# RMS norms summed into full banks on every partition, with the opening's work and its weight panels in a new order

## The reference

```python
def _rmsnorm(x, w):
    xf = x.astype(jnp.float32)
    y = xf * lax.rsqrt(jnp.mean(xf * xf, axis=-1, keepdims=True) + EPS)
    return (y * w.astype(jnp.float32)).astype(x.dtype)

def prep(t, use_rope):        # the first mixer, for the tokens and for the context
    rq, rk, rv, rg, mq, mk, mv, mo, mg = jnp.split(t @ w_in, AB_SPLITS, axis=-1)
    ...                       # heads, rope on rq and rk, a short convolution on mq and mk, gates
```

## Time and profile before

| | us |
|---|---|
| median of 3 runs (2335.64 to 2337.13) | 2336.91 |
| the profiled execution | 2333.99 |
| its span | 2332.2 |
| PE busy | 2236.8 (96%) |
| DVE busy | 1052.4 (45%) |
| ACT busy | 449.4 (19%) |
| POOL busy | 110.2 (5%) |

### The profile page before, as it was taken

How to read it: one execution, slowest core, us unless ns; L and a number is a source line. 1 busy time by engine, 2 the same in 40 slices (tenths; PEclk the granted TensorE clock), 3 DMA queues, 4 the chain that set the end, 5 groups by cost and what they waited for, 6 DMA issues and landing times.

```text
span 2332.2 us, 39035 instructions
## 1 busy us (share of the span) xinstructions
PE 2236.8 (96%) x16791; PEld 1627.1 (70%) x16791; DVE 1052.4 (45%) x2007; ACT 449.4 (19%) x1063; POOL 110.2 (5%) x103
## 2 busy tenths in 40 slices
PE   6989999999999999999999989999999999999997
PEld 4434454478886786678888668888775877777775
DVE  5488465478888335854431454441334520000001
ACT  1310242200000003630000351000332321111101
POOL 0210120000000420000000000000003000000000
PEclk9999999999999999999999999999999899999999
DMA  8424632244554324037885416886534158899994
GB/s 286 161 97 144 214 112 73 72 145 145 174 188 116 97 95 154 1 109 252 293 266 154 150 61 216 288 277 175 189 109 146 46 194 323 301 331 330 331 345 181
DMA packets 306217, 428.13 MB, mean 184 GB/s; under 512 B 11604, under 2 KB 166867, under 8 KB 305803
## 3 DMA queue, kind: packets, MB, share of 16 engines
q1 hardware_dynamic: 303412, 422.55, 53.2%
q10 hardware_dynamic: 2646, 3.26, 0.4%
HBM read 424.55 MB, written 1.13 MB: 183 GB/s over the span
## 4 chain that ended last, share of the span: by engine, by line
PE 90%; DVE 6%; ACT 1%; issue 1%; DMA 1%; ACTq 0%; SPq 0%; DVEq 0%
PE banks L645 76%; PE banks L905 3%; DVE mem L1846 2%; PE banks L654 1%; ACT mem L2871 1%; DVE mem L1849 1%; PE banks L1635 1%; PE banks L1039 1%; PE banks L1459 1%; DVE mem L1842 1%; PE banks L1074 1%; DVE mem L2438 1%; PE banks L1699 1%; PE banks L869 1%; PE banks L1081 0%
## 5 line engine op out<-in xcount | busy, mean ns | idle before, releaser
L645 PE MATMUL banks<-mem 128*32 128x128 f32 (+5 forms) x12722 | 1817.1, 359 | 21.6 <-ACT mem L2871 10.9
L645 PEld LDWEIGHTS banks<-mem 128*128 128x128 f32 (+3 forms) x12722 | 1308.2, 148 | 502.8 <-issue 296.6
L1846 DVE SCALAR_TENSOR_TENSOR mem<-mem 128x512 f32<-128x512 f32 (+4 forms) x523 | 376.9, 746 | 22.1 <-DMA mem<-mem 7.8
L2871 ACT ACTIVATE mem<-banks 128x256 f32<-128x256 f32 (+8 forms) x383 | 152.1, 419 | 1103.1 <-PE banks L645 804.3
L2871 ACT ACTIVATE mem<-mem 128x256 f32<-128x256 f32 (+11 forms) x445 | 192.0, 482 | 662.0 <-DVE mem L1846 469.5
L1849 DVE TENSOR_TENSOR mem<-mem,banks 128x256 f32<-128x256 f32 (+3 forms) x88 | 43.3, 492 | 561.8 <-ACT mem L2871 536.6
L1846 DVE SCALAR_TENSOR_TENSOR mem<-banks,mem 128x256 f32<-128x256 f32 (+7 forms) x258 | 133.6, 543 | 344.8 <-PE banks L645 227.5
L1849 DVE TENSOR_TENSOR mem<-mem 128x256 f32<-128x256 f32 (+13 forms) x272 | 153.5, 576 | 35.2 <-ACT mem L2871 19.8
L1849 DVE TENSOR_TENSOR mem<-banks,mem 128x256 f32<-128x256 f32 (+3 forms) x224 | 90.9, 410 | 101.9 <-PE banks L645 43.9
L654 PE MATMUL banks<-mem 128*128 128x128 f32 (+2 forms) x391 | 61.1, 293 | 24.1 <-DMA mem<-in_ctx 11.3
L654 PEld LDWEIGHTS banks<-mem 128*128 128x128 f32 (+2 forms) x391 | 46.0, 150 | 51.0 <-issue 22.8
(11 more groups left out here) (180 smaller groups left out, 826.6 us busy)
## 6 DMA issues: line engine op xcount, KB each, us to landing
mem<-in_ada_w SPq DMA_DIRECT2D x96, 1024.0 KB, 9.9
mem<-in_moe_w_gate_up SPq DMA_DIRECT2D x64, 1024.0 KB, 10.7
mem<-in_ffn_w_in SPq DMA_DIRECT2D x44, 1024.0 KB, 6.9
mem<-in_moe_w_down SPq DMA_DIRECT2D x48, 768.0 KB, 7.4
mem<-in_moe_w_gate_up SPq DMA_DIRECT2D x32, 768.0 KB, 12.6
mem<-in_ffn_w_out SPq DMA_DIRECT2D x32, 704.0 KB, 6.8
mem<-in_ffn_w_gate_up SPq DMA_DIRECT2D x22, 1024.0 KB, 6.4
mem<-in_ab_w_in SPq DMA_DIRECT2D x16, 1024.0 KB, 9.5
```

The lines of the kernel that those rows point to most:

```text
L645: ins = nc.tensor.matmul(o, lhsT, rhs, start=start, stop=stop)
L1846: return V.scalar_tensor_tensor(out=o, in0=a, scalar=sc, in1=b, op0=op0, op1=op1)
L2871: ac = lambda o, i, f, **k: nc.scalar.activation(o, i, f, **k)
```

## The change

- **Norms.** `norm_sum` now has the ones (128x128) as the stationary operand and the squares as the moving one, so that every partition gets the sums of all tokens in a full bank. Root and inverse run over all tokens (512 or 256 columns) on 128 partitions. `norm_spread` and the small matmul that opened the bank are gone; the scaling reads the inverse from `rms` (the former `rstd`) in place of a bank. The gain is computed ahead of the inverse.
- **Opening.** ACT squares each block as soon as it is copied, ahead of the SiLU. PE sums each of the eight squares itself (`sum_squares`, into bank 7), four of them between the last transposes and four after the packs; DVE's additions are gone. Both ada panels run back to back after that, and their two transposes follow each other. ACT loads the table for the root ahead of time.
- **Panels.** No ada panel is loaded or accumulated in the third panel (n = 2). Each later one moves one place back, and the last panel (n = 7) has two: one is summed after its second tile, and the accumulation of the other runs on DVE after that.

Left out of the diff: names of semaphores and counters, the rename of `rstd`, the other calls of `norm_spread`, and a second bank cleared at the start.

```diff
...
@@ -536,9 +536,9 @@
                 some_adas(2)
                 plain(w_in, [(512, 512), (4096, 32)])
                 some_adas(1)
-                for cc in (1024, 2048, 2560, 1536, 3584, 3072):
+                for cc, n in ((1024, 0), (2048, 1), (2560, 1), (1536, 2), (3584, 1), (3072, 2)):
                     plain(w_in, [(cc, 512)])
-                    some_adas(2 if cc == 1536 else 1)
+                    some_adas(n)
                 plain(A["ab_w_out"][0], [(0, 512), (512, 512)])
                 def spread_ctx(h):
...
@@ -728,26 +728,16 @@
             def norm_sum(width, src=hT, added=True, ends=(0, 7)):
-                m, tiles = c["nsq"], width // P
+                m = c["nsq"]
                 if added:
                     await_("norm_added", "nadd")
-                nc.tensor.matmul(PS[3][:, 0:tiles], const("ones", (HD, P)), const("ident", (HD, P))[:, 0:tiles], start=True, stop=True)
                 for k in (0, 7) if added else range(KD):
                     if k or not added:
                         pe.wait_ge(s["norm_squared"], m.n + k + 1)
-                    for i in range(tiles):
-                        b = ends[k // 7] if added else k
-                        last = nc.tensor.matmul(PS[3][:, i:i + 1], src[:, b, i * P:(i + 1) * P], const("ones")[:, 0:1],
-                                                start=False, stop=k == KD - 1, skip_group_check=True)
+                    b = ends[k // 7] if added else k
+                    last = nc.tensor.matmul(PS[3][:, 0:width], const("ones"), src[:, b, 0:width], start=k == 0, stop=k == KD - 1)
                 last.then_inc(s["sum_ready"], 1)
                 m.n += KD
-
-            def norm_spread(width):
-
-                await_("norm_inverted", "rooted")
-                for i in range(width // P):
-                    nc.tensor.matmul(PS[6 + i // 2][:, i % 2 * P:i % 2 * P + P], rstd[:, i:i + 1].to_broadcast([P, P]), ident,
-                                     start=True, stop=True).then_inc(s["norm_spread"], 1)
             pending = []
@@ -943,7 +933,7 @@
                     pe.wait_ge(s["blk_taken"], done + 3)
                     product(e, weights_of(w, 1, 1, q), blk.t4, more=True).then_inc(s["blk_ready"], 1)
-            def turn_x():
+            def turn_x(after):
                 pe.wait_ge(s["x_loaded"], 32)
                 for k in range(8):
@@ -952,22 +942,31 @@
                     for t in range(4):
                         last = turn(PS[k % 4][:, t * P:(t + 1) * P], xin[:, t, k * P:(k + 1) * P])
                     last.then_inc(s["x_turned"], 1)
+                    after(k)
+
+            def sum_squares(k):
+
+                pe.wait_ge(s["norm_squared"], k + 1)
+                last = mm(PS[7][:, :], const("ones"), hT[:, k, :], k == 0, k == 7)
+                if k == 7:
+                    last.then_inc(s["sum_ready"], 1)
+                    c["nsq"].n += KD
             pe.wait_ge(s["const_loaded"], 16)
-            turn_x()
+            turn_x(lambda k: sum_squares(k - 4) if k >= 4 else None)
             pe.wait_ge(s["vectors_loaded"], NVEC * 16)
             for g, pack in enumerate(PACKS):
                 n = sum(x for _, x in pack)
                 last = turn(PS[6][:, g * P:g * P + n], pack_rows[0:n, g, :])
             last.then_inc(s["packs_turned"], 1)
+            for k in range(4, 8):
+                sum_squares(k)
             pe.wait_ge(s["cond_ready"], 4)
-            ada()
-            ada_turned(2, c["ada"].n)
-            norm_sum(T2)
-            ada()
-            ada_turned(3, c["ada"].n)
+            for _ in range(2):
+                ada()
+            for i in (2, 3):
+                ada_turned(i, c["ada"].n - 1)
             if stop >= 1:
-                norm_spread(T2)
                 w = panel(8, 512)
                 def unshifted(b, after=lambda k: None):
@@ -1001,7 +1000,7 @@
                             project(w, slice(b * P, (b + 1) * P), T2)
                         else:
                             project_tok(w, b, slice(0, 512), 512)
-                        if n == 5 and b == 1:
+                        if n in (5, 7) and b == 1:
                             ada_sum(2, beside=True)
                         if n == 2:
@@ -1020,7 +1019,8 @@
                     if n == 1:
                         w = panel(8, 32)
                         project(w, slice(0, 32), T2, rows=(0, 32))
-                    ada_sum(2)
+                    if n != 2:
+                        ada_sum(2)
                 def spread_from(col):
...
@@ -1919,13 +1912,12 @@
             def last_adas():
-                ada_copied(3)
-                ada_biased(3)
+                for i in (2, 3):
+                    ada_copied(i)
+                for i in (2, 3):
+                    ada_biased(i)
             def norm(par, which, weight, parts, final=False, between=None):
-                await_("norm_rooted", "sum")
-                tiles = 2 * parts
-                V.reciprocal(rstd[:, 0:tiles], rstd[:, 0:tiles]).then_inc(s["norm_inverted"], 1)
                 if between:
                     between()
                 dve.wait_ge(s["ada_taken"], c["ada"].n)
@@ -1933,16 +1925,14 @@
                     nw = weight.unsqueeze(2).to_broadcast([P, KD, parts])
                     link(stt(gain[:, :, 0:parts], mod[:, par, 24 * which + 8:24 * which + 16, 0:parts], 1.0, nw,
                              ALU.add, ALU.mult))
-                dve.wait_ge(s["norm_spread"], c["spread"].n + 2)
+                await_("norm_rooted", "sum")
+                link(V.reciprocal(rms[:, 0:parts * L], rms[:, 0:parts * L]))
                 for k in range(KD):
                     for j in range(parts):
-                        if k == 0 and j:
-                            dve.wait_ge(s["norm_spread"], c["spread"].n + tiles)
                         t = slice(j * L, (j + 1) * L)
                         g = weight[:, k:k + 1] if final else gain[:, k, j:j + 1]
-                        stt(hT[:, k, t], xT[:, k, t], g, PS[6 + j][:, 0:L], ALU.mult, ALU.mult).then_inc(s["scaled"], 1)
+                        stt(hT[:, k, t], xT[:, k, t], g, rms[:, t], ALU.mult, ALU.mult).then_inc(s["scaled"], 1)
                         c["scaled"].next()
-                c["spread"].n += tiles
             def add_out(par, which, parts, m, early=None):
...
@@ -2175,10 +2166,7 @@
                 V.tensor_copy(pack_cols[:, g, 0:n], PS[6][:, g * P:g * P + n]).then_inc(s["packs_copied"], 1)
             dve.wait_ge(s["packs_copied"], 4)
             dve.wait_ge(s["const_loaded"], 16)
-            ada_copied(2)
-            ada_biased(2)
-            for m in range(8):
-                add_square(m, T2, hT)
+            c["nsq"].n += KD
             def rope(dst, bank, tmp):
@@ -2188,7 +2176,16 @@
             if stop >= 1:
-                norm(0, 0, col("norm_w", 0, 8), 2, between=last_adas)
+                await_("norm_rooted", "sum")
+                V.reciprocal(rms, rms)
+                last_adas()
+                dve.wait_ge(s["ada_taken"], c["ada"].n)
+                link(stt(gain, mod[:, 0, 8:16, :], 1.0, col("norm_w", 0, 8).unsqueeze(2).to_broadcast([P, KD, 2]), ALU.add, ALU.mult))
+                for k in range(KD):
+                    for j in range(2):
+                        t = slice(j * L, (j + 1) * L)
+                        stt(hT[:, k, t], xT[:, k, t], gain[:, k, j:j + 1], rms[:, t], ALU.mult, ALU.mult).then_inc(s["scaled"], 1)
+                        c["scaled"].next()
                 more = [0]
                 def ada_next():
@@ -2239,14 +2236,13 @@
                     rope(qk[:, b, 0:L], bank, rope_tmp).then_inc(s["proj_taken"], 1)
                     dve.wait_ge(s["proj_taken"], c["proj"].n)
-                ada_next()
+                c["panels"].n += 1
                 dve.wait_ge(s["proj_taken"], 9)
                 for t in range(4):
                     bank = item()
                     V.tensor_copy(rv[:, t, :], bank[:, :]).then_inc(s["proj_taken"], 1)
                     rotate(t)
                     rotate(4 + t)
-                ada_end()
                 await_("act_for_dve", "act")
                 link(stt(fg, fg, 0.0, mrow, ALU.min, ALU.subtract))
                 one = const("ones", (0, 8))[:, 0:1]
@@ -2292,6 +2288,9 @@
                     if t == 0:
                         dve.wait_ge(s["proj_taken"], c["proj"].n - 1)
                     V.tensor_copy(mv[:, t, :], bank[:, :]).then_inc(s["proj_taken"], 1)
+                    if t == 1:
+                        ada_end()
+                        ada_acc(0, 2)
                 ada_end()
                 def ret_gate(p):
@@ -2896,15 +2895,15 @@
                 await_("mean_ready", "mean")
                 ac(v, v, ACT.Sqrt).then_inc(s["rstd_ready"], 1)
-            def norm_root(tiles):
+            def norm_root(width):
                 await_("sum_ready", "norms")
```

(24 more changed lines are left out.)

## The result

The changed kernel takes 2342.42 us (median of 15 runs, 2338.57 to 2347.76), the kernel before 2335.60 (15 runs): 1.0031 of it, interval 1.0024 to 1.0039, 6.8 us slower. The forecast was 2344.6, and 7.7 us slower on the profiled execution; the profiled executions differ by 2340.65 - 2333.99 = 6.66.

A forecast was written before the change was run, and what follows sets the result against it. TensorE was taken as the bound, 90% of the chain of waits. Terms -4.5 - 10.2 + 9 + 2 + 4.9 + 5.5 + 1 = +7.7 on 2333.99 gave 2341.7, plus 2.92 for the median 2344.6 us; 8 in 10: 2335 to 2352.

The forecast's parts named there:

- opening: Start of the kernel to the first scaling: scaling starts at about 31.1 in place of 35.76; -4.5 us (-3 to -5.5).
- third panel: Rotations in the third panel: with DVE free, the fourth pair begins at 136.72, not 146.96; -10.2 us (-7.3 to -11).
- first units' stall and low clock: First retention units: late spreads delay ACT's square and DVE's gate, +9 us (4 to 14); low clock after, +2 (0 to 2.8).
- norms, root to scaling: Seven later norms: longer root and inverse, +4.9 us for five at 256 tokens, +5.5 for two at 512.
- norms, low clock: Behind the later norms: PE is idle longer, so the low clock may last longer; +1 us (0 to 5).
- Its rival: Third panel: PE waits for DVE all the same, some 7 of the 10.2 us stay, about 2351; chance 0.08.
- 13.3 and 19.8: First units, spreads' issue to five heads exponentiated: 13.3 us as before, or 6.5 us more if behind the `ab_w_out` load.
- the 11.4 us: First units: the stall if the spreads' data comes after the 2.1 MB of `ab_w_out`, against 4.9 us otherwise.
- The 4.27 us: Norms: a 512-column inverse by the skill page's estimate; the forecast used the profile row's 3.354 us instead.
- early spreads: Rival, first units: spreads don't queue behind `ab_w_out`, stall 4.9 us or less, total about 2337.5; chance 0.24.

## Why the prediction was right

The sign and the size held, 2342.4 for 2344.6; the waits fell where they were told, and no rival came about. That the sum came within 1 us is luck in part: in the traces the stall and the low clock behind it were 1.9 smaller than forecast and the kernel before lost 1.3 of its own at 396, while the opening gave 0.6 less and the norms cost 1.7 more. Third panel and stall together were to lose 0.8 and won 1.2 (1.6 alone, interval -4.0 to +0.7). The terms, in us:

| term | forecast | the two traces | runs |
|---|---|---|---|
| opening | -4.5 | -3.9 | -5.6 (alone) |
| third panel | -10.2 | -10.3 | |
| first units' stall and low clock | +9 +2 | +7.4 +1.7 | |
| third panel and stall together | +0.8 | -1.2 | -1.6 (alone) |
| units to the first later norm (low clock at 396 in before only) | none | -1.3 | |
| norms, root to scaling | +4.9 +5.5 | +5.2 +5.6 | +11.2 (clock filled in both) |
| norms, low clock | +1 | | about +2 |
| norms together, to the end | +11.4 | +13.1 | +9.6, +14.2, +12.8 |
| sum | +7.7 | +6.7 | +6.8 |

**Opening.** The mechanism was right and the direct gain was 5.4, at the upper bound: the inverse ended at 25.73 + 3.35 = 29.08 (forecast 29.3), and PE started 1.02 us behind the first scaling in the kernel before, which puts the scaling here at 30.3 (forecast 31.1): the two copies, transposes, biases and the gain took 1.2 us, where I had estimated 1.4 to 2.0. In this trace 1.5 of it was lost again in the first ada sum. I had said that PE's idle time ahead of it moves along, which it did, but not that the clock might fall behind it; it did so in some of the traces of either opening, and alone the opening measured 5.6 (3.5 to 7.7).

**Third panel.** Right to 0.1 us. Its rival, that PE waits for DVE all the same, would have shown idle time between the rotations, and there is none.

**First units.** The place, the waits and the order of the queue were as told. The term was 1.6 too large in the stall. The square was free 9.33 us after the units' start in the kernel before, and the heads were done 0.6 + 16.2 us after it; 16.8 - 9.33 = 7.5, which is the stall. I had bounded the 16.2 by 13.3 and 19.8, the upper one with 6.5 us for the panel. The panel's packets did take 6.2 us, but the spreads' first packet, which came 0.96 us after the issue in the kernel before, came 5.97 after it here, 5.0 later, and the first mask followed it by 1.8 us in place of 2.7: 4.1 later in all (7.8 against 3.65). Then POOL had five heads in one piece of 6.90 us, where in the kernel before it waited for a spread twice in between and took 8.11: 1.2 back, and 13.3 + 4.1 - 1.2 = 16.2. The Trainium skill (DMA: Bandwidth & Descriptors, section Queues, rings and completion order) has descriptors consumed in the ring's order on each DMA engine. The trace agrees: the spreads' first packet starts at 283.70, the panel's last one ends at 283.95. Only the 11.4 us that I had put beside it were too many.

**Norms.** Root to scaling was 2.37 and 4.17, forecast 2.30 and 4.11. The inverse of 512 columns took 3.35 us in the opening and in the norms, as the earlier trace rows had it. The 4.27 us estimated from the Trainium skill (VectorE: DVE Perf Modes, section First, the fixed hardware budget) were too many. One sum of a rival is off by a little: with +0.2 the early spreads end at 2337.1, not 2337.5.

**The low clock.** +1 (0 to 5) for the norms was nearly right for the difference: filling PE's idle time gave 13.1 us with wide norms (13.3 with the spreads first) and 10.3 with the old ones (11.7), so 1.6 to 2.8 more, less than the runs can tell apart from none. What I did not see is that both kernels paid ten or more. The earlier trace rows showed 0.56 behind one norm, and I used it only to say that it may last longer.

**What stays open.** The three ways to price the wide norms without idle products give 9.6, 14.2 and 12.8 us. Their intervals overlap; whether they cost more beside the new opening or whether low clock merely fell out differently was not settled.

## What to carry to other kernels

When work is moved out of a place where it stalls TensorE, follow every DMA that was issued behind it: most of the third panel's 10 us went back in the first units since a 2 MB load had come to stand ahead of five small ones, and swapping them in the queue gave 6.1 and 4.7 us in two kernels. A root and an inverse over all tokens on all partitions are no saving where TensorE waits for them: a few columns and a spread take 1.3 us, 512 columns 4.2. And before one shortens a wait of TensorE by a microsecond, look at the clock behind it: here some 10 us lay behind seven waits of 1.2 to 1.3, and products into a free bank brought them back, although the clock still fell at a few of these norms.

## What was not expected of the hardware

- After 1.2 to 1.3 us of idle PE in a norm of the kernel before the clock read 0.50 to 0.63 over the first 3 us of the projection behind six of the seven, as it read 0.50 after 5.79 us. But not always: of the kernel before, behind the third and the fourth norm at 256 tokens,

```profile
1415.60:1418.60 3.00, 3.00 (x14) 2.66 (x15) 2.96 (x8) 2.98 (x8) 0.00 (x0) 1.00 0.31 57
1655.70:1658.70 3.00, 3.00 (x8) 0.94 (x9) 2.03 (x6) 2.98 (x8) 0.00 (x0) 0.50 0.27 35
```

  with the same 1.27 us of idle time ahead of both. In the same way the 2.42 us ahead of the first ada sum were followed by a low clock in the changed kernel and by 4.30 us at the full one in the kernel with the old norms and the spreads first. So a loss of 1.5 us came and went at one place.
- With PE idle for 0.63 to 1.00 us ahead of each projection, in the changed kernel with idle products, it read 1.00 behind all seven. In the old norms with products around the spread it fell at the first norm at 512 tokens to 0.63 over 433.00 to 435.85, with no idle time of PE above 0.34 us since 426. So idle time alone does not tell when it falls; what else does was not tried.
- A panel of whole rows moved at 393 to 400 GB/s. One row broadcast to 128 partitions moved at 399 (285 to 286 us of the changed kernel) and at 203 to 224 in other windows, with the DMA share at 1.0 in all of them; a packet of 3072 bytes took 0.13 us in the first and 0.22 to 0.25 in the others. What slows it was not settled. POOL's masks run beside it in the slow windows, but also at 397 GB/s (291 to 292 us of the kernel with the spreads first).
